# First layer of a two-block network on one core: k, v and the first queries from h without adaLN's shift

## Chip, cores and metric

One core of one Trainium2 chip runs the whole program. The metric is the device time of one execution in microseconds; the table below gives three of them and the one that was profiled.

## Reference

The input x is 256 tokens by 2048 columns, in float32, and there are 256 context tokens of the same width. A first block has two layers, a second block one (a gated spatial and recurrent mix, and a feed-forward part in three pieces); the change is in the first block. Cut to what matters:

```python
shift, scale, gate = jnp.split(jax.nn.silu(c) @ ada_w[l] + ada_b[l], 3, axis=-1)
shift_c, scale_c, gate_c = jnp.split(jax.nn.silu(c_ctx) @ ada_w[l] + ada_b[l], 3, axis=-1)
h = rmsnorm(x, norm_g[l]) * (1.0 + scale[:, None]) + shift[:, None]
hc = rmsnorm(xc, norm_g[l]) * (1.0 + scale_c) + shift_c
q, k, v, up, uf, g = split_proj(h @ w_in[l])     # and the same of hc
```

q and k get a norm per head and, for x's tokens, rope; attention of 8 heads in 2 key groups over 512 keys follows; up and uf go through a pooling and a Fourier mix; the three are joined, multiplied with silu(g), and projected by w_out. Since h is a scaled part plus one row per source, h @ W is the scaled part times W, plus shift @ W added to every row.

## The kernel before

**Chunks.** All weights stream from DRAM in chunks of 512 KB (128 partitions x 1024 float32) through 8 buffers, RAW, loaded in order by SyncE's queue. A chunk of w_in or w_out is split in two float32r parts, SPL (4 buffers): ScalarE copies the high part (L1329), VectorE subtracts to get the low part (L1555), and TensorE does three matmuls (high x high, high x low, low x high) for each product. A chunk of ada_w isn't split: TensorE multiplies it in float32 by the two columns of silu(c) (CW), two matmuls of 128x512 for a chunk, each shown as two records (L1113). Eight chunks of ada_w are one group of 512 of adaLN's 6144 values; a group's result is copied out (ada_out, L1339), turned with TensorE (ada_turn, L1181) and added up on VectorE into the columns ADA. Of the 12 groups of a layer, 0 to 3 are the shift, 4 to 7 the scale and 8 to 11 the gate.

**Buffers come free** at different moments: a RAW buffer of a split chunk when VectorE has taken its low part, one of an ada chunk only when TensorE has multiplied it. A load waits in SyncE's queue for the buffer eight chunks back, with every later load behind it.

**The order** of all engines' work is one list, written when the program is built. `run_chunks` walks the chunks; before each it takes pieces of small work from the list `hi` (or `low`, for attention rows), as many as the chunk group's `side` says: norms, tiles of h, attention, pooling, squares. Every engine does its part of the list in order, so an engine that waits holds all that follows. `run_ahead` places a chunk's split 5 chunks ahead of its multiplication (AHEAD), at the start 3 (START_AHEAD, for the first 72 chunks). Ada chunks that aren't needed at once lie in the list `left`, and `mixed` lays them between the chunks of a projection, two after every second one.

**The start** (`start`, `main`): 64 ada chunks of layer 0, scale and shift of one quarter of the columns at a time, with the 8 chunks of the k and v projection (kv) between them; then q0, q1 (queries), gp (pool), gf (Fourier) and the gates, with `left` between. In between, x and ctx are loaded, turned by TensorE into columns (turn_x, L1167, 16 times, copied by VectorE, L1566), and the mean squares give the row scale (rstd_a, rstd_b: L1572, L1950, L1577, L1174). A tile of h (128 columns of one source, 256 tokens) takes three steps: h0 on VectorE scales (L1599), h1 on ScalarE adds the shift and rounds to the high part (L1347), h2 on VectorE makes the low part (L1604). In layer 1, h1 has a second pass on ScalarE (L1350) and h2 runs on GpSimd (L1959). A chunk of kv, or of the first layer's projections, is 24 matmuls of 512 columns (L1132 to L1134, or L1146 to L1148); in layer 1's q0, q1, gp and gf it is 12.

**kv to q0.** When kv is done, kv_out empties `hi`, in which `load_tables` (three small loads on ScalarE's DMA queue, L1356 to L1358) and `tables` (VectorE, L1615 to L1618) stand, and then copies k to QS and v to VT (L1365, L1371, L1626), which lie where the columns of x were, once these are spilled to DRAM (L1945). q0 uses the same four banks of PSUM. Then the norms run (n0, n1, n2) and attention units of four steps: scores (L1196), softmax, turned probabilities (L1203), times v (L1213).

**Between the layers**, 8 ada chunks (FILL) are laid after w_out's last: four, then the count of the squares (L1265), four more, then the row scale (L1174) and layer 1's first tiles of h.

Of the kernel before, what the change touches and what calls it, by code (L numbers as in the profile page):

```python
# [5 lines left out]
F32 = mybir.dt.float32  # L6
# [15 lines left out]
FILL = 8  # L22
# [35 lines left out]
def two_block_program(nc, I, out):  # L58
    es = ExitStack()
    with es:  # L60
# [57 lines left out]
        gate = lambda l, k, s: ADA[:, l, 32 + k, s:s + 1]  # L118
        V = lambda c: VV[:, c:c + 1]
# [62 lines left out]
        s_h0, s_h1, s_h1b, s_h2 = sem("h_scaled"), sem("h_hi"), sem("h_shifted"), sem("h_lo")  # L182
# [124 lines left out]
        def run_chunks(upto):  # L307
            while at["pos"] < upto:
# [4 lines left out]
                if c.shape == 0:  # L313
                    pop_side(2 if c.group.side == 2 and c.kc % 2 == 0 else 0)
# [5 lines left out]
                ks = {0: [], 2: range(2 * c.kc, 2 * c.kc + 2), 4: range(4 * c.kc, 4 * c.kc + 4)}[c.shape]  # L320
# [3 lines left out]
                for part in range(parts):  # L324
                    if part:
                        pop_side(c.group.side)
# [17 lines left out]
        def mixed(main, left):  # L344
            seq = []
            for c in main:
                seq.append(c)
                if len(seq) % 4 == 2:
                    seq.extend(left[:2])
                    del left[:2]  # L350
            return seq
# [5 lines left out]
        ada_ready, s2_ready = {}, {}  # L357

        def ada_group(l, g, side=0):
            def after():  # L360
# [5 lines left out]
                hi.insert(1, lambda: spread(slot))  # L366

            def spread(slot):
                s = put("ada_turn", slot=slot, l=l, g=g, after=use(7))
# [63 lines left out]
        def tile_h(l, k, s, x, done):  # L433
            y = {}

            def s0():
                y["slot"], last = take()
                y["h"] = put("h0", l=l, k=k, s=s, slot=y["slot"], last=[x["rs"], s2_ready[l, k // 4], *last])["n"]
                bank_last[5] = [(s_h0, y["h"])]

            def s1():
                y["h"] = put("h1", l=l, k=k, s=s, slot=y["slot"], scaled=y["h"], last=[ada_ready[l, k // 4], *x["ended"]])["n"]
                y["again"] = tick("h1b") if l else 0

            def s2():
                h = put("h2", l=l, k=k, s=s, slot=y["slot"], hi=y["h"], again=y["again"])
# [4 lines left out]
        def layer(l):  # L451
            both, lv = l == 0, lay[l]
            W = I["w_in"][l, :, :]
            h, x = {}, {"qs": [], "ended": [], "maps": [[(s_colT, 3)], [(s_colT, 3)]]}
# [6 lines left out]

            def need_x(k):
# [4 lines left out]
            need["kv", l] = need_both  # L467
# [18 lines left out]
            def rows_out(banks, width, queries=False):  # L486
# [3 lines left out]
                elif both or x.get("qs_used"):  # L490
                    flush(hi)
                x["qs_used"] = True
                s = put("rows_out", l=l, banks=banks, width=width, last=[multiplied(), *x["qs"]], a=count.get("qa", 0), d=count.get("qd", 0))
                x["qs"] = []
# [6 lines left out]
            def norm_item(i, nh, which, tt, ready, dest):  # L501
                y = {}
                rope = tt[0] == 0

                def s0():
                    slot, last = take()
                    s = put("n0", l=l, i=i, nh=nh, slot=slot, last=[ready, *last])
                    give(slot, (s_nred, s["n"]))

                def s1():  # L510
                    (a, last), (c, more) = (take(), take()) if rope else ((None, []), (None, []))
                    s = put("n1", l=l, i=i, nh=nh, which=which, t=tt[1], rope=rope, a=a, c=c, last=last + more + [x["tables"]], rope_n=tick("rope") if rope else 0)
# [4 lines left out]
                def s2():  # L517
                    bk = 5 if both else 7
                    s = put("n2", l=l, i=i, nh=nh, dest=dest, bank=bk, after=use(bk))
                    bank_last[bk] = [(s_nev, s["n"])]  # L520
                    x["qs"].append((s_ntr, s["n"]))
                    x["qk"] = (s_nev, s["n"])
                return [s0, s1, s2]

            def kv_out():
# [5 lines left out]
                for b in range(4):  # L531
                    bank_last[b] = [(s_v, 4 * s["n"] - 3 + b)]
                hi.extend(staged([norm_item(i, 2, 1, tt, ready[i], lv.KTr[:, :, i * 128:(i + 1) * 128]) for i, tt in enumerate(TILES)]))
                if not both:
                    hi.append(lambda: low.extend([unit_row] * (2 * len(us) + 3)))
# [156 lines left out]
            kv = group("tm", ("kv", l), W, 1024, [0, 1, 2, 3], kv_out, TILES)  # L692
# [1404 lines left out]
```

## Time and profile before

| what | value |
|---|---|
| median of 3 runs | 2458.5 us (2456.53 to 2460.01) |
| profiled execution | 2454.96 us, its span 2453.2 us |
| busy in the span | PE 2324.8 us (95%), DVE 1291.5 (53%), ACT 1043.2 (43%), POOL 197.1 (8%) |
| DMA | 436.66 MB, mean 178 GB/s |
| a load of ada_w, of w_in | 512 KB each, x192 and x208 |

The span runs from the first to the last instruction; the profiled execution's own time is 1.8 us more. PE is TensorE's matmul, DVE VectorE, ACT ScalarE, POOL GpSimd, SP SyncE; a q behind the name is the engine's queue, where loads are issued. Matmuls overlap each other, so a row's length (0.39 us) is more than the distance between two starts (0.23 us), and it is the starts that are to be counted.

### The profile page before, as it was taken

Reading aid. Unit: us, or ns where it says so; the run is one execution under the profiler, and the core shown is the slowest. Engines: PE = TensorE matmul, PEld = TensorE weight load, DVE = VectorE, ACT = ScalarE, POOL = GpSimd, SP = SyncE. Lnnn points to the kernel's source line nnn. Section 1 sums busy time; section 2 is a strip of 40 time slices with the busy share of each in tenths; the row PEclk is TensorE's granted clock in tenths of the full one; section 3 lists DMA queues with packets and bytes.
Section 4 is the critical chain, followed back from the end, with each engine's and each line's share of the span. In section 5 each row is a group of like instructions: output and inputs, shape, how many; then the busy total and the mean of one; then the engine's idle time right before and its main releaser. Section 6 shows DMA issues by size and latency. Waiting matters only on the chain.

```text
span 2453.2 us, 30580 instructions
## 1 busy us (share of the span) xinstructions
PE 2324.8 (95%) x12135; PEld 1861.9 (76%) x12135; DVE 1291.5 (53%) x2110; ACT 1043.2 (43%) x1596; POOL 197.1 (8%) x237
## 2 busy tenths in 40 slices
PE   5889999999999979899989988989999999999998
PEld 2467777677777657678877867868888888888887
DVE  2444533142332263545666776557665676567664
ACT  2232333342321263445544545445543555345543
POOL 1000100000010131100021014120000000000001
PEclk8999999999999999999989999989999999999999
DMA  9864433335655565534555554646655655565652
GB/s 367 294 236 172 142 120 124 123 112 171 232 172 172 202 221 208 167 102 147 187 157 171 180 172 130 189 132 186 189 181 188 189 183 186 186 186 186 188 184 83
DMA packets 347021, 436.66 MB, mean 178 GB/s; under 512 B 13848, under 2 KB 269280, under 8 KB 345984
## 3 DMA queue, kind: packets, MB, share of 16 engines
q1 hardware_dynamic: 341376, 413.19, 51.8%
q0 software_dynamic: 3408, 16.38, 1.9%
q10 hardware_dynamic: 2096, 5.15, 0.6%
q8 instruction: 96, 1.57, 0.3%
q14 instruction: 45, 0.37, 0.0%
HBM read 428.37 MB, written 6.29 MB: 177 GB/s over the span
## 4 chain that ended last, share of the span: by engine, by line
PE 85%; DVE 5%; ACT 4%; DMA 3%; issue 2%; POOL 1%; SPq 0%; ACTq 0%; POOLq 0%; DVEq 0%
PE ps L1151 32%; PE ps L1152 16%; PE ps L1146 5%; PE ps L1148 5%; PE ps L1147 5%; PE ps L1132 4%; PE ps L1134 4%; PE ps L1133 4%; PE ps L1113 3%; ACT SPL L1329 2%; DVE SPL L1555 2%; PE ps L1196 1%; PE ps L1213 1%; DMA RAW<-in_w_in_dram 1%; DMA RAW<-in_ada_w_dram 1%
## 5 line engine op out<-in xcount | busy, mean ns | idle before, releaser
L1151 PE MATMUL ps<-HS,SPL 128*128 128x512 f32 x3456 | 1236.1, 402 | 16.9 <-POOL HS L2007 16.1
L1555 DVE TENSOR_TENSOR SPL<-RAW,SPL 128x1024 fp32r<-128x1024 f32 x592 | 726.4, 1233 | 669.4 <-ACT SPL L1329 667.3
L1152 PE MATMUL ps<-HS,SPL 128*128 128x256 f32 x3456 | 973.6, 282 | 0.0
L1329 ACT ACTIVATE SPL<-RAW 128x1024 fp32r<-128x1024 f32 x592 | 621.7, 1057 | 536.1 <-PE ps L1152 356.5
L1151 PEld LDWEIGHTS ps<-HS,SPL 128*128 128x128 f32 x3456 | 654.6, 189 | 183.4 <-POOL HS L2007 16.9
L1152 PEld LDWEIGHTS ps<-HS,SPL 128*128 128x128 f32 x3456 | 658.2, 190 | 2.1 <-issue 1.9
L1132 PE MATMUL ps<-SPL,HS 128*128 128x512 f32 x576 | 248.5, 431 | 30.1 <-ACT XT L1371 8.5
L1134 PE MATMUL ps<-SPL,HS 128*128 128x512 f32 x576 | 228.5, 397 | 0.0
L1133 PE MATMUL ps<-SPL,HS 128*128 128x512 f32 x576 | 228.4, 396 | 0.0
L1146 PE MATMUL ps<-HS,SPL 128*128 128x512 f32 x512 | 212.2, 414 | 1.2 <-DVE HS L1711 1.2
L1148 PE MATMUL ps<-HS,SPL 128*128 128x512 f32 x512 | 200.5, 392 | 0.0
L1147 PE MATMUL ps<-HS,SPL 128*128 128x512 f32 x512 | 200.2, 391 | 0.0
L1132 PEld LDWEIGHTS ps<-SPL,HS 128*128 128x128 f32 x576 | 110.4, 192 | 79.6 <-issue 22.1
L2002 POOL TENSOR_TENSOR TMP<-TMP 128x256 f32<-128x256 f32 (+1 forms) x68 | 61.6, 905 | 1240.5 <-ACT TMP L1463 1238.0
L1133 PEld LDWEIGHTS ps<-SPL,HS 128*128 128x128 f32 x576 | 110.8, 192 | 26.6 <-issue 6.0
L1146 PEld LDWEIGHTS ps<-HS,SPL 128*128 128x128 f32 x512 | 96.6, 189 | 43.9 <-issue 16.1
L1134 PEld LDWEIGHTS ps<-SPL,HS 128*128 128x128 f32 x576 | 110.3, 192 | 24.8
L1113 PE MATMUL ps<-RAW,CW 128*32 128x512 f32 x768 | 113.6, 626 | 11.2 <-DMA RAW<-in_ada_w_dram 9.1
L1463 ACT ACTIVATE TMP<-XT 128x256 f32<-128x256 f32 (+1 forms) x72 | 33.5, 465 | 191.9 <-DVE XT L1723 124.1
L1147 PEld LDWEIGHTS ps<-HS,SPL 128*128 128x128 f32 x512 | 96.7, 189 | 22.4 <-issue 3.8
L1148 PEld LDWEIGHTS ps<-HS,SPL 128*128 128x128 f32 x512 | 96.4, 188 | 21.1
L1908 DVE SCALAR_TENSOR_TENSOR MM<-MM,VV 128x256 f32<-128x256 f32 x192 | 80.0, 478 | 0.0
(251 smaller groups left out, 1543.7 us busy)
## 6 DMA issues: line engine op xcount, KB each, us to landing
RAW<-in_w_in_dram SPq DMA_DIRECT2D x208, 512.0 KB, 5.6
RAW<-in_ada_w_dram SPq DMA_DIRECT2D x192, 512.0 KB, 4.9
RAW<-in_ffn_w_up_dram SPq DMA_DIRECT2D x192, 512.0 KB, 3.6
RAW<-in_w_out_dram SPq DMA_DIRECT2D x96, 512.0 KB, 4.5
RAW<-in_ffn_w_down_dram SPq DMA_DIRECT2D x96, 512.0 KB, 3.4
x_spill<-XT POOLq DMA_DIRECT2D x2, 2048.0 KB, 14.8
XT<-x_spill POOLq DMA_DIRECT2D x1, 4096.0 KB, 15.8
MM<-in_x_dram ACTq DMA_DIRECT2D x2, 1024.0 KB, 10.8
```

What stands on the lines that cost most here:

```text
L1113: m = mm(PS[6][32 * q:32 * q + 32, :], CW[:, 2 * k:2 * k + 32], raw_of(i)[:, kk * 512:(kk + 1) * 512], start=kc < 2, stop=kc >= 6, skip_gr ...
L1132: mm(PS[b][:, :], hr, wr, start=k == 0, stop=False, skip_group_check=True)
L1133: mm(PS[b][:, :], hr, wl, start=False, stop=False, skip_group_check=True)
L1134: m = mm(PS[b][:, :], hl, wr, start=False, stop=k == KT - 1, skip_group_check=True)
L1146: mm(PS[b][:, :], wr, hr, start=k == 0, stop=False, skip_group_check=True)
L1147: mm(PS[b][:, :], wr, hl, start=False, stop=False, skip_group_check=True)
L1148: m = mm(PS[b][:, :], wl, hr, start=False, stop=k == KT - 1, skip_group_check=True)
L1151: mm(PS[b][:, :], wr, hh, start=k == 0, stop=False, skip_group_check=True)
L1152: m = mm(PS[b][:, 256:512], wl, hh[:, 0:256], start=False, stop=k == KT - 1, skip_group_check=True)
L1329: act(SPL[:, (n - 1) % NSPL, 0, :], raw_of(i), ACT.Copy).then_inc(s_hi, 1)
L1555: tt(w[:, 1, :], raw_of(s["i"]), w[:, 0, :].bitcast(F32), ALU.subtract).then_inc(s_lo, 1)
L1908: stt(o, CV[c][:, tap:tap + 256], V(c_fw[tap] + col), o, ALU.mult, ALU.add).then_inc(s_ct, 1)
```

## The change

It does the following.

1. kv and q0 of layer 0 read a "bare" h: scaled and split, without the shift (`tile_h`, ACT.Copy in h1). So `start` holds only the four scale groups (32 ada chunks) and kv. The four shift groups move behind it (`go_on`), between the 8 chunks of q0, and when a quarter of the shift is there, `shift_h` adds it to that quarter's tiles: the same three steps again for the 32 tiles, from the high and low parts.
2. The missing part of k, v and q0 is a row: `shift_rows` multiplies the shift columns with the chunks of w_in's columns 1024 to 1535 and 0 to 511, **loaded a second time**: 16 more chunks in ada form, laid between q1's chunks, two after each. The row is spread over the tokens by two float32 matmuls of 512 columns for each of the two groups, and VectorE adds it to the four tiles of rows, which wait in BARE (MM's memory). k's norms come after the first, q0's after the second; attention starts behind that.
3. `kv_out`'s emptying of `hi` is gone for layer 0: kv's banks are copied at once, in full width; `load_tables` and `tables` stand in `hi` behind the last tiles of h.
4. h2 of layer 1 goes from GpSimd to VectorE, and the second ScalarE pass of h1 goes.
5. START_AHEAD now holds to chunk 80. In layer 0 from q1 on, a half chunk takes a piece of `hi` and one of `low`, no longer one of them. During the first scale group six pieces are taken at every second chunk, no longer two.
6. `left` is laid out anew: none between q1's chunks, two after each chunk of w_out (before: after every second), FILL is 16, and none remains for layer 1's projections, which had 24.

```diff
-FILL = 8
+FILL = 16
+        BARE = [MV[:, i, 8:16, :].rearrange("p k n -> p (k n)").rearrange("p (t c) -> p t c", t=4) for i in range(2)]
-            while at["taken"] < min(len(queue), at["pos"] + (START_AHEAD if at["pos"] < 72 else at["ahead"])):
+            while at["taken"] < min(len(queue), at["pos"] + (START_AHEAD if at["pos"] < 80 else at["ahead"])):
...
+                    hi.insert(1, lambda: add(slot, s["n"]))
+                def add(slot, out):
+                    while "scr_a" not in x:
+                        hi.pop(0)()
+                    s = put("shift_rows", which=which, slot=slot, out=out, ready=x["bare"][which], last=x["scr_a"], after=use(4, 5))
...
-            kv = group("tm", ("kv", l), W, 1024, [0, 1, 2, 3], kv_out, TILES)
-            q0 = group("tm", ("in", l), W, 0, qb[0], q_out(0, qb[0]), lv.tiles, 1 if both else 2)
+            kv = group("tm", ("kv", l), W, 1024, [0, 1, 2, 3], bare_out(0) if both else kv_out, TILES)
+            q0 = group("tm", ("kv", l), W, 0, qb[0], bare_out(1), TILES) if both else group("tm", ("in", l), W, 0, qb[0], q_out(0, qb[0]), lv.tiles, 1 if both else 2)
...
-                cs = ada_group(0, 4 + u, 2) + ada_group(0, u, 2)
+                cs = ada_group(0, 4 + u, 2 if u else 6)
...
-                return cs[:12] + kv[2 * u - 2:2 * u - 1] + cs[12:] + kv[2 * u - 1:2 * u] if u else cs
+                return cs[:4] + kv[2 * u - 2:2 * u - 1] + cs[4:] + kv[2 * u - 1:2 * u] if u else cs
+            def go_on(u):
+                c = q0[2 * u + 1]
...
+                    hi.extend(staged([shift_h(k, s, bare, h, used) for k in range(4 * u, 4 * u + 4) for s in range(2)]))
...
+                cs = ada_group(0, u, 2)
+                return cs[:4] + q0[2 * u:2 * u + 1] + cs[4:] + [c]
...
-                main = [c for u in range(4) for c in start(u)] + kv[6:8], q0 + q1 + gp + gf + gates
+                main = ([c for u in range(4) for c in start(u)] + kv[6:8] + [c for u in range(4) for c in go_on(u)]
+                        + mixed(q1, shift_rows(0) + shift_rows(1), 1)), gp + gf + gates
...
-        lay_out(mixed(outs0, left))
+        lay_out(mixed(outs0, left, 1))
...
-        run_chunks(marks[1] + FILL // 2)
-        at["ahead"] = 2
+        run_chunks(marks[1] + 6)
...
-        run_chunks(marks[2])
+        run_chunks(marks[1] + 12)
+        flush(hi)
+        at["ahead"] = AHEAD
...
-                    if l:
-                        e.wait_ge(s_h1, n)
-                        act(t, t, ACT.Identity, bias=shift(l, k, src)).then_inc(s_h1b, 1)
...
+                elif kind == "shift_rows":
+                    for sm, v in new((s_sel, 16)):
+                        e.wait_ge(sm, v)
+                    e.wait_ge(s_adaE, s["out"])
+                    for src in range(2):
+                        m = mm(PS[4 + src][:, :], SPREAD[:, src, :], T(s["slot"]), start=True, stop=True, skip_group_check=True)
+                    m.then_inc(s_sp, 1)
```

## Rows read from the trace of the kernel before

**Rows 1.** Page of the profile: busy us of each engine, share of the span, instructions.

```profile
PE 2324.8 (95%) x12135; PEld 1861.9 (76%) x12135; DVE 1291.5 (53%) x2110; ACT 1043.2 (43%) x1596; POOL 197.1 (8%) x237
```

**Rows 2.** Windows table: us, busy us of each engine, granted clock, DMA share, GB/s.

```profile
20.00:40.00 20.00, 16.53 (x91) 6.61 (x88) 6.62 (x17) 5.20 (x6) 0.00 (x0) 0.71 1.05 390
0.00:160.00 160.00, 112.61 (x567) 60.64 (x568) 58.69 (x139) 44.34 (x70) 12.47 (x26) 0.90 0.91 331
210.00:272.00 62.00, 61.26 (x309) 46.06 (x307) 32.87 (x69) 22.38 (x42) 4.93 (x4) 1.00 0.38 135
845.00:1000.00 155.00, 132.68 (x630) 92.69 (x622) 77.96 (x136) 73.55 (x122) 36.66 (x41) 0.96 0.64 223
```

**Rows 3.** Timeline, 20 to 75 us: start, length, engine, line, tile, wait.

```profile
23.78 1.91 ACT L1334 ACTIVATE HS<-MM 128x2048 fp32r<-128x2048 f32 x1 [1.27 <-DMA MM<-in_ctx_dram]
...
32.94 1.09 PE L1167 MATMUL ps<-IDN,MM 128*128 128x128 f32 x8
...
34.96 1.09 PE L1167 MATMUL ps<-IDN,MM 128*128 128x128 f32 x8
...
58.69 0.68 DVE L1566 COPY XT<-ps 128x512 f32<-128x512 f32 x1
...
66.26 0.47 PE L1132 MATMUL ps<-SPL,HS 128*128 128x512 f32 x1 [0.65 <-DVE HS L1604]
...
72.80 1.93 PE L1113 MATMUL ps<-RAW,CW 128*32 128x512 f32 x16
```

**Rows 4.** Timeline of TensorE, 118 to 137 us.

```profile
121.69 0.50 PE L1132 MATMUL ps<-SPL,HS 128*128 128x512 f32 x1 [2.65 <-DVE SPL L1555]
...
127.36 1.92 PE L1113 MATMUL ps<-RAW,CW 128*32 128x512 f32 x16
...
129.21 0.50 PE L1132 MATMUL ps<-SPL,HS 128*128 128x512 f32 x1
```

**Rows 5.** Timeline, 140 to 163 us, and landing times of GX's small loads.

```profile
143.55 0.53 ACTq L1358 DMA_DIRECT2D GX<-in_k_norm_g_dram  x1
...
153.38 0.43 DVE L1615 TENSOR_TENSOR XT<-TMP,GX 128x256 f32<-128x256 f32 x1 [10.33 <-DMA GX<-in_k_norm_g_dram]
...
155.15 0.75 DVE L1626 COPY XT<-ps 128x256 f32<-128x256 f32 x2
...
156.79 0.77 PE L1132 MATMUL ps<-SPL,HS 128*128 128x512 f32 x1 [8.12 <-ACT XT L1371]
...
161.19 0.52 PE L1133 MATMUL ps<-SPL,HS 128*128 128x512 f32 x1
...
DMA to landing us min/median/max: 5.2/7.2/9.8
```

**Rows 6.** Timeline of TensorE, 205 to 215 us: q1's first matmul.

```profile
208.99 0.47 PE L1132 MATMUL ps<-SPL,HS 128*128 128x512 f32 x1 [0.59 <-DVE XT L1626]
```

**Rows 7.** Chain that ended last, 230 to 250 us and 780 to 860 us.

```profile
240.11 0.86 PE ps L1196 x2
...
820.63 1.00 PE ps L1113 x8
...
832.73 1.00 PE ps L1113 x8
```

**Rows 8.** Timeline, 830 to 860 us: the boundary between the two layers.

```profile
849.48 0.88 SPq L1080 DMA_DIRECT2D RAW<-in_w_in_dram  x2
...
853.04 1.06 ACT L1329 ACTIVATE SPL<-RAW 128x1024 fp32r<-128x1024 f32 x1 [5.36 <-DMA RAW<-in_w_in_dram]
...
858.38 0.47 PE L1132 MATMUL ps<-SPL,HS 128*128 128x512 f32 x1 [2.26 <-POOL HS L1959]
```

**Rows 9.** Who waited for whom on TensorE: us in total, times, longest us.

```profile
PE ps L1132 <- POOL HS L1959: 7.0, 5, 3.8
```

**Rows 10.** Timeline of VectorE, 104 to 130 us: two steps of h.

```profile
107.85 0.48 DVE L1599 SCALAR_TENSOR_TENSOR TMP<-XT,S,ps 128x256 f32<-128x256 f32 x1
...
108.24 0.48 DVE L1604 SCALAR_TENSOR_TENSOR HS<-TMP,ADA,HS 128x256 fp32r<-128x256 f32 x1
```

More of the change, by code:

```diff
@@ L313, in run_chunks @@
                 if c.shape == 0:
[L314 removed]
+                    pop_side(c.group.side if c.kc % 2 == 0 else 0)
                 elif c.group.side == 0:
@@ L324, in run_chunks @@
                 for part in range(parts):
-                    if part:
+                    if part and c.group.side == 0:
+                        pop_pair()
+                    elif part:
                         pop_side(c.group.side)
@@ L342, in staged, with mixed @@
             return [row(r) for r in range(len(tasks) + depth - 1)]
-        def mixed(main, left):
+        def mixed(main, left, every=2):
             seq = []
[L346 to L350, printed above, removed]
+            for i in range(0, len(main), every):
+                seq.extend(main[i:i + every] + left[:2])
+                del left[:2]
             return seq
@@ L357, in two_block_program, with need_shift @@
         ada_ready, s2_ready = {}, {}
+        need["ada"] = lambda k: [(s_c, 1)]
+        def need_shift(k):
+            while any((0, g) not in ada_ready for g in range(4)):
+                hi.pop(0)()
+            return [ada_ready[0, g] for g in range(4)]
+        need["shift"] = need_shift
         def ada_group(l, g, side=0):
@@ L460, in need_both, with need_bare @@
                 return [h[k, 0], h[k, 1]]
+            def need_bare(k):
+                while (k, 1) not in bare or (k, 0) not in bare:
+                    hi.pop(0)()
+                return [bare[k, 0], bare[k, 1]]
             def need_x(k):
@@ L465, in need_x @@
                 return [h[k, 0]]
-            need["kv", l] = need_both
+            need["kv", l] = need_bare if both else need_both
             need["in", l] = need_both if both else need_x
@@ L489, in rows_out, with copy_rows @@
                         hi.pop(0)()
-                elif both or x.get("qs_used"):
+                elif x.get("qs_used"):
                     flush(hi)
                 x["qs_used"] = True
-                s = put("rows_out", l=l, banks=banks, width=width, last=[multiplied(), *x["qs"]], a=count.get("qa", 0), d=count.get("qd", 0))
-                x["qs"] = []
+                while "tab" not in x:
+                    hi.pop(0)()
+                last, x["qs"] = [multiplied(), *x["qs"]], []
+                return copy_rows(banks, width, [lv.QS[:, i, 0:width] for i in range(len(banks))], last)
+            def copy_rows(banks, width, dest, last):
+                put("rows_out", banks=banks, width=width, dest=dest, last=last)
                 ready = []
@@ L506, in s0 @@
                     slot, last = take()
-                    s = put("n0", l=l, i=i, nh=nh, slot=slot, last=[ready, *last])
+                    s = put("n0", l=l, i=i, nh=nh, rows=xq, slot=slot, last=[ready, *last])
                     give(slot, (s_nred, s["n"]))
@@ L511, in s1 @@
                     (a, last), (c, more) = (take(), take()) if rope else ((None, []), (None, []))
-                    s = put("n1", l=l, i=i, nh=nh, which=which, t=tt[1], rope=rope, a=a, c=c, last=last + more + [x["tables"]], rope_n=tick("rope") if rope else 0)
+                    s = put("n1", l=l, i=i, nh=nh, rows=xq, which=which, t=tt[1], rope=rope, a=a, c=c, last=last + more + [x["tables"]], rope_n=tick("rope") if rope else 0)
                     if rope:
@@ L724, in start_h, with add_shift @@
                         put("spill", last=[multiplied()])
[L725 to L726 removed]
+                    hi.extend(staged([tile_h(0, k, s, x, bare) for k in range(4 * u, 4 * u + 4) for s in range(2)])
+                              + ([lambda: put("select_in"), load_tables, tables, load_dft] if u == 3 else []))
                 cs[-1].then = start_h
[L728 removed]
+                return cs[:4] + kv[2 * u - 2:2 * u - 1] + cs[4:] + kv[2 * u - 1:2 * u] if u else cs
+            def go_on(u):
+                c = q0[2 * u + 1]
+                after_q = c.then
+                def add_shift():
+                    while (0, u) not in ada_ready:
+                        hi.pop(0)()
+                    used = multiplied()
+                    hi.extend(staged([shift_h(k, s, bare, h, used) for k in range(4 * u, 4 * u + 4) for s in range(2)]))
+                    if after_q:
+                        after_q()
+                c.then = add_shift
+                cs = ada_group(0, u, 2)
+                return cs[:4] + q0[2 * u:2 * u + 1] + cs[4:] + [c]
             def begin():
```

130 lines of the change are left out of this document (93 added, 37 removed).

## The prediction

> **What bounds the kernel now.** The page comes first: TensorE is busy for 2324.8 of 2453.2 us, VectorE for 1291.5 [rows 1], so time is won where TensorE stands idle and lost where its work grows. The windows table says where: in the first 160 us it is busy for 112.6, at a mean granted clock of 0.90, while DMA is 0.91 busy; from 210 to 272 us it is busy for 61.3 of 62.0; from 845 to 1000 us, where layer 1 begins, for 132.7 of 155 [rows 2]. So there is idle time at the start and in layer 1, and next to none between. The timelines say why. The first kv matmul comes at 66.26 us, since the columns of x are turned a few at a time between ada chunks (last copy at 58.69) [rows 3]; then 64 ada chunks have to be loaded, twice as many as the scale needs; and at the end of kv VectorE waits 10.3 us for a small load, and TensorE 8.1 us behind it [rows 5].
>
> **The start.** The last part of ctx is there at 23.8 us. Two turns and two ada chunks take 2.02 us now, a pair of turns alone 1.09 [rows 3]. Sixteen turns with six chunks between them so take between 8.7 and 16.2 us; I take 12.5, nearer the mixed row. From the last copy to the first matmul it is 7.6 us (58.69 to 66.26) [rows 3], and the scale's last group has to be turned first (1.1 us). So kv begins at 23.8 + 12.5 + 7.6 + 1.1 = 45.0 us.
>
> From there TensorE sets the pace. A kv chunk takes 5.67 us, a block of four ada chunks 1.85 [rows 4], together 7.52; their five loads take 5 x 1.34 = 6.7 us at 390 GB/s [rows 2]. DMA keeps up, with 10% to spare. The first chunk takes 6.5 us [rows 3], then come five times 7.52, three turns of a group (0.6 each), 1.8 us of waiting for the last quarter's tiles (an estimate: two tiles, each two steps 0.395 apart [rows 10]) and two more kv chunks: 45.0 + 6.5 + 37.6 + 1.8 + 1.8 + 11.3 = 104.0 us.
>
> Here the stall of kv's end is **kept, and grows**. By my count of the pieces, `load_tables` and `tables` are both taken at the first ada chunk behind kv, and kv's copies stand before them. ScalarE copies two banks of 512 columns (1.3 us; two of 256 take 0.75) and issues three loads (the last takes 0.53, so 1.6), that one lands 5.2 to 9.8 us later, VectorE works on the tables for 1.8 us (153.4 to 155.2) [rows 5], and q0's first split (1.2 us) stands behind that in VectorE's order. I take 7.2 for the landing, the middle of the loads read: the deep queue of spill and loads that gave 9.8 is mostly gone by then. q0 begins at 104.0 + 1.3 + 1.6 + 7.2 + 1.8 + 1.2 = 117.1 us; with four ada chunks done in between, TensorE idles for 11.2 us. Before, 8.1.
>
> The Trainium skill (DMA: Bandwidth & Descriptors, "Queues, rings and completion order") says that each DMA engine serves the queues in turn, packet by packet, so a small load on ScalarE's queue needn't wait until SyncE's large ones are through. The 9.8 us of the trace speak against relying on it. By that rule the landing would be at the short end, and the sum 2 us lower.
>
> q0: eight chunks, seven blocks of four, four turns of a group, and 2.2 us for the lower clock after the stall, as from 156.79 to 161.19 us, where starts are 0.43 us apart and no longer 0.23 [rows 5]: 45.4 + 13.0 + 2.4 + 2.2 = 63.0. With 0.7 us for the first copy, q1 begins at 180.8 us, and not at 208.99 [rows 6]: 28.2 us earlier. What was done by then and now isn't goes off: four pairs of `left` and k's turns (1.2 us). Two ada chunks are 1.00 us busy; with the change to and fro I price a pair at 1.2, since two pairs in w_out's stage are 12.10 us apart, with 48 matmuls 0.227 apart between them [rows 7]. So 28.2 - 4.8 - 1.2 = **22.2 us won**. The second set of 32 tiles costs VectorE 32 x 2 x 0.395 = 25 us and ScalarE 16 [rows 10]; it lies beside q0's 63 us, where VectorE otherwise has 10 of splits. I cost it at nothing; uncovered, it would hold q1.
>
> **What is added.** The 16 chunks of w_in loaded again go between q1's chunks, where TensorE is full [rows 2]: eight pairs, **9.6 us lost**. DMA has 135 GB/s there and hides them. Spreading the rows: four float32 matmuls of 512 columns at 0.86 (scores have that shape) [rows 7], **3.4 lost**. VectorE's additions (some 6 us) lie beside q1 and gp. The attention rows now start in gp's last chunk; the last that a gate wants (unit 32, row 35) is taken some 20 half chunks before need, so I put nothing for them.
>
> **`left`.** The gates lose eight pairs, w_out's stage gains sixteen, both full [rows 2, 7]: **9.6 lost**. The fill gains eight chunks, layer 1's projections lose twelve pairs: **14.4 won** if TensorE sets the pace there.
>
> **The boundary.** Fills 8 to 15 can be loaded only when fills 0 to 7 are multiplied, and layer 1's first chunk of w_in comes behind them. From the first fill (about 849 us) a load takes 3.6 us to the split (849.5 to 853.04 [rows 8]), eight more are ahead at 1.34: 863.3, plus 2.6 of split is 865.9, and not 858.38: **7.5 lost**.
>
> **h2 on VectorE.** TensorE's waits for GpSimd's h2 go, **7.0 won** [rows 9]. VectorE then needs 2 x 2 x 0.395 + 1.23 = 2.8 us for a chunk of q0 with x's tiles alone, about TensorE's 2.8 (half of 5.67), but 4.4 where ctx's tiles are made too, in four chunks (6.8 us over), and the tables (2.3) stand before them: **9.1 lost**. The windows row's clock of 0.96 over 155 us [rows 2] means 6 us lost to low clock; with shorter pauses I give 2.3 back. Layer 1 with its boundary: -14.4 + 7.5 - 7.0 + 9.1 - 2.3 = -7.1.
>
> **Sum:** -22.2 + 9.6 + 3.4 + 9.6 - 7.1 = -6.7 us. Against the profiled execution's 2454.96 this is 2448.3; that one lies 3.5 below the median of the three runs, and I carry the difference to the median: 2452 us.
>
> **Bounds.** Turns -3.8 to +3.7; landing -2.0 to +2.6; a pair 1.0 to 1.4, with 16 more pairs in full stages, 3 either way; layer 1's VectorE from nothing (-9) to as much again (+7); the start's loads: at the 331 GB/s mean of the first 160 us [rows 2] five loads take 7.9 us and not 6.7, 0.4 more than TensorE's 7.52, 13 times: +5.
>
> **Rivals.**
> A. *The start pays in full and VectorE keeps up in layer 1.* Landing 5.2 us, turns at their short end, no shortage by h2: 2452 - 2 - 3.8 - 9.1 = 2437 us. For it: VectorE is busy for 78 of 155 us there [rows 2]. Against: its work comes in bursts in front of need. 0.22.
> B. *Slower: the pairs moved out of layer 1 are paid twice.* While idle time there comes from the in-order splits and tiles of h, ada chunks fill it for nothing; in w_out's stage each pair costs 1.2. It decides once VectorE's 4.4 us for a chunk stands against TensorE's 2.8: then the 14.4 us don't come back, and the time is 2452 + 14 = 2466 us. For it: TensorE idles 22 us there with these fillers in. Against: k and v's eight chunks of 5.67 leave VectorE ample time, so their four pairs do come back. 0.22.
> C. *The start stays bound by its loads.* Twice four of eight buffers wait for TensorE's multiplications, the spill falls into kv's end, and q1 begins near 191, not 181: 2462 us. 0.12.
> D. *It doesn't do what it says*, as tables that hold q0 until the spill is done, or h that is late for q1, eat the start's gain: 2458, no change. 0.06.
> The forecast has 0.38, with 2445 to 2459 as its own range.
>
> **How the numbers follow.** A measurement of this kernel can tell about 0.2%, 4.9 us, from no change. Faster by more (under 2453.6): A and 0.25 of the forecast's 0.38, together 0.47. Within: 0.13 of the forecast, D, and parts of B and C, 0.27. Slower (over 2463.4): most of B and half of C, 0.26. The range, 2436 to 2468, takes in A's and B's times.
>
> **What would show it.** In the profile after: first kv matmul near 45 us; a wait of VectorE for GX's load and one of TensorE of 10 to 12 us behind it near 105 to 117 us; q1 near 181; the ada line with 832 records (208 chunks of four), no longer 768; TensorE full from q1 to w_out; layer 1's first matmul 21 us after w_out's last, no longer 14; TensorE waiting there for VectorE's h. I am wrong if q1 begins before 172 or after 190, if the boundary costs under 3 us, or if layer 1's stretch from there to the pool projection is shorter than before by more than 12 us.

## The result and the profile after

| | before | after |
|---|---|---|
| median of the runs compared | 2459.26 us (2456.53 to 2463.38) | 2489.74 us (2483.93 to 2495.43) |
| span of the profiled execution | 2453.2 us | 2482.1 us |

The ratio is **1.0137, 95% interval 1.0109 to 1.0165**: slower by 30 us, outside the range. The runs below were compared in later groups, each against its own runs of the kernel before (medians 2456.13, 2454.69, 2455.32, 2453.45), so ratios are what to compare.

The windows table of the profile after (columns as in [rows 2]) has the start better and the rest worse:

```profile
0.00:160.00 160.00, 119.24 (x631) 77.40 (x635) 70.38 (x167) 47.55 (x80) 12.38 (x26) 0.96 0.84 301
186.00:642.00 456.00, 446.76 (x2132) 327.20 (x2130) 171.26 (x342) 142.23 (x242) 22.60 (x25) 1.00 0.42 140
845.00:1000.00 155.00, 122.43 (x513) 85.17 (x512) 77.39 (x144) 47.71 (x72) 8.10 (x7) 0.86 0.53 176
```

The timeline of the start, after. kv begins 21.2 us sooner than in [rows 3], TensorE's wait in front of q0 is longer than in [rows 5], and q1 comes 23.3 us sooner than in [rows 6]:

```profile
45.09 0.47 PE L1219 MATMUL ps<-SPL,HS 128*128 128x512 f32 x1 [2.16 <-DVE HS L1703]
...
115.09 0.43 DVE L1729 TENSOR_TENSOR XT<-TMP,GX 128x256 f32<-128x256 f32 x1 [8.50 <-DMA GX<-in_k_norm_g_dram]
...
118.21 0.76 PE L1219 MATMUL ps<-SPL,HS 128*128 128x512 f32 x1 [11.09 <-DVE SPL L1650]
...
134.42 0.42 ACT L1443 ACTIVATE HS<-TMP 128x256 fp32r<-128x256 f32 x1 [5.54 <-PE ps L1221]
134.75 1.04 ACT L1424 ACTIVATE SPL<-RAW 128x1024 fp32r<-128x1024 f32 x1
137.10 0.50 PE L1219 MATMUL ps<-SPL,HS 128*128 128x512 f32 x1 [0.92 <-DVE SPL L1650]
...
142.45 1.06 ACT L1424 ACTIVATE SPL<-RAW 128x1024 fp32r<-128x1024 f32 x1 [1.30 <-DMA RAW<-in_w_in_dram]
...
185.73 0.47 PE L1219 MATMUL ps<-SPL,HS 128*128 128x512 f32 x1 [1.64 <-DVE MM L1740]
```

The timeline of TensorE at the boundary, after, which answers to [rows 8]. The first row is w_out's last matmul, the last one layer 1's first. Between them lie 18 ada chunks, not 16: the last pair that is laid among w_out's chunks stands behind its last matmul (863.12), and the turn of its group waits for its copy before the first fill starts at 866.73. The kernel before has the same, and so 10 chunks there and not 8:

```profile
862.80 0.39 PE L1235 MATMUL ps<-HS,SPL 128*128 128x512 f32 x1
863.12 1.06 PE L1200 MATMUL ps<-RAW,CW 128*32 128x512 f32 x8
866.17 0.63 PE L1276 MATMUL ps<-IDN,TMP 128*128 128x128 f32 x4 [1.99 <-ACT TMP L1434]
866.73 4.48 PE L1200 MATMUL ps<-RAW,CW 128*32 128x512 f32 x24
...
874.83 3.93 PE L1200 MATMUL ps<-RAW,CW 128*32 128x512 f32 x16 [0.74 <-ACT TMP L1434]
...
884.08 3.28 PE L1200 MATMUL ps<-RAW,CW 128*32 128x512 f32 x8 [1.66 <-DMA RAW<-in_ada_w_dram]
892.48 1.08 PE L1276 MATMUL ps<-IDN,TMP 128*128 128x128 f32 x4 [5.12 <-ACT TMP L1434]
893.21 0.77 PE L1219 MATMUL ps<-SPL,HS 128*128 128x512 f32 x1
```

The same timeline of the kernel before, from w_out's last matmul to the first matmul of layer 1's gates, and that second matmul after:

```profile
844.45 0.39 PE L1148 MATMUL ps<-HS,SPL 128*128 128x512 f32 x1
...
1063.84 0.79 PE L1151 MATMUL ps<-HS,SPL 128*128 128x512 f32 x1
```

```profile
1099.30 0.79 PE L1238 MATMUL ps<-HS,SPL 128*128 128x512 f32 x1
```

With the start of ScalarE's first pass for w_out (647.04 before, 642.70 after) the path falls into four stretches, and they say where the time went:

| stretch | before | after | difference | I had predicted |
|---|---|---|---|---|
| start to w_out | 647.0 | 642.7 | -4.3 | -18.8 |
| w_out, to its last matmul | 197.4 | 220.1 | +22.7 | +19.2 |
| to layer 1's first matmul | 13.9 | 30.4 | +16.5 | +7.5 |
| to layer 1's gates | 205.5 | 206.1 | +0.6 | -14.6 |

Together +35.5 at layer 1's gates; the rest is 6.6 us shorter, for no reason in the change: that tail is 1381 to 1391 us long in all profiled executions here, in no order with the edits. (The last column puts each term of the prediction in the stretch that it lies in.)

### The profile page after: what moved, and what is told of

It is laid out like the page before. It is cut to its first block, busy times and chain, and to the rows that moved or that the text cites. A ratio compares the mean times of both kernels' runs of the same rounds, so it can differ in the third digit from the quotient of the medians.

```text
span 2482.1 us, 30820 instructions
## 1 busy us (share of the span) xinstructions
PE 2335.6 (94%) x12207; PEld 1864.3 (75%) x12207; DVE 1330.8 (54%) x2218; ACT 1036.7 (42%) x1592; POOL 172.6 (7%) x206
## 4 chain that ended last, share of the span: by engine, by line
PE 84%; DVE 6%; ACT 4%; issue 2%; DMA 2%; POOL 1%; ACTq 0%; POOLq 0%; DVEq 0%
PE ps L1238 31%; PE ps L1239 15%; PE ps L1233 5%; PE ps L1234 5%; PE ps L1235 5%; PE ps L1219 4%; PE ps L1221 4%; PE ps L1220 4%; PE ps L1200 3%; ACT SPL L1424 2%; DVE SPL L1650 2%; PE ps L1291 1%; PE ps L1308 1%; PE ps L1298 1%; PE ps L1334 1%
## 5 line engine op out<-in xcount | busy, mean ns | idle before, releaser
L1238 PE MATMUL ps<-HS,SPL 128*128 128x512 f32 x3456 | 1229.1, 400 | 17.9 <-POOL HS L2121 16.9
L1219 PE MATMUL ps<-SPL,HS 128*128 128x512 f32 x576 | 247.7, 430 | 35.7 <-DVE SPL L1650 14.4
L1200 PE MATMUL ps<-RAW,CW 128*32 128x512 f32 x768 | 106.7, 628 | 4.6 <-ACT CW L1414 2.0
```

The lines of the kernel that those rows point to most:

```text
L1200: m = mm(PS[6][32 * q:32 * q + 32, :], vec, raw_of(i)[:, kk * 512:(kk + 1) * 512], start=kc < 2, stop=kc >= 6, skip_group_check=True)
L1219: mm(PS[b][:, :], hr, wr, start=k == 0, stop=False, skip_group_check=True)
L1238: mm(PS[b][:, :], wr, hh, start=k == 0, stop=False, skip_group_check=True)
```

## The experiments

**Undo the layout of `left`** (e1_left). Fillers are the ada chunks laid between others. Here 24 are back in layer 1's projections, 48 between w_out's chunks and not 64, FILL and the boundary's code as before.

```diff
-FILL = 16
+FILL = 8
-        lay_out(mixed(outs0, left, 1))
+        for i, c in enumerate(outs0):
+            seq.append(c)
+            if i % 4 < 3:
+                seq.extend(left[:2])
+                del left[:2]
...
-        run_chunks(marks[1] + 6)
+        run_chunks(marks[1] + FILL // 2)
+        at["ahead"] = 2
```

> The changed kernel with layer 1's fillers put back: FILL 8 with the old code at the boundary, 24 chunks of left in layer 1's projections again, and so 48 instead of 64 between w_out's chunks. Theory (the boundary and the missing fillers lose most of layer 1's 19 us): w_out's last matmul to layer 1's first falls from 30.4 us to 14 to 16, w_out's stage is 9 us shorter, layer 1 gets 12 pairs back of which its idle time takes a half, in all 12 to 20 us faster than the changed kernel, 2470 to 2478 us. Rival (h2 on VectorE is the cause of layer 1's loss): the boundary still falls, but layer 1's stretch grows by the whole 12 to 14 us, in all no more than 8 us faster. Rival of the record (pairs are paid wherever they lie): the same time for left, only the boundary gains.

Measured: 2460.02 us, a ratio to the kernel before of 1.0020 (1.0010 to 1.0031). By the ratios the layout alone is 29 of the 34 us lost, and more than the 12 to 20 I expected. Its boundary is 13.1 us long, and its layer 1, 24 fillers richer, 200.2 us, no longer than after's.

**Undo the move of h2**, alone (e2_pool) and together with the above (e3_both): h1's second pass on ScalarE and h2 on GpSimd again.

```diff
+                        act(t, t, ACT.Identity, bias=shift(l, k, src)).then_inc(s_h1b, 1)
...
-                elif kind == "h2":
...
+                elif kind == "h2" and s["l"] == 0:
...
+                    e.wait_ge(s_h1b, s["again"])
+                    tt(HX(1, k, src, 1), T(s["slot"])[:, 0:256], HX(1, k, src, 0).bitcast(F32), ALU.subtract).then_inc(s_h2, 1)
```

> The changed kernel with layer 1's h2 back on GpSimd and h1's second pass back on ScalarE. Theory (the boundary and fillers): VectorE is relieved of 32 x 0.4 = 13 us, TensorE's waits for h (7.6 us) and for the norms (12.9 us) shrink to those of the kernel before (7.0 and 7.0), 3 to 7 us faster than the changed kernel; the boundary stays at 28 us or more. Rival (h2 on VectorE is the cause): 12 us or more faster.

> Both together: what is left of the change is layer 0's start, the shift rows, and a row of attention per half chunk. Theory: about the sum of the two alone, 15 to 25 us faster than the changed kernel, 2465 to 2475 us, so still slower than the kernel before by 6 us or more, because the 16 extra chunks and 9 us of waits in q1, gp and gf eat what the start wins. Rival (the whole loss is in layer 1): at or below 2459 us.

Measured: 2493.4, 1.0158 (1.0143 to 1.0173), and 2462.82, 1.0023 (1.0007 to 1.0039). Nothing is won by undoing it, where I had expected 3 to 7 us for it alone; if anything it is a little worse. Who waited for whom on TensorE, 860 to 1010 us, after and then with h2 on GpSimd: the wait for h changes its name and hardly its length.

```profile
PE ps L1283 <- DVE MM L1770: 10.6, 2, 5.6
PE ps L1219 <- DVE HS L1705: 7.6, 5, 2.3
PE ps L1276 <- ACT TMP L1434: 7.1, 2, 5.1
PE ps L1219 <- DVE MM L1740: 4.6, 1, 4.6
```

```profile
PE ps L1284 <- DVE MM L1770: 11.8, 2, 6.1
PE ps L1220 <- POOL HS L2073: 9.8, 7, 3.6
PE ps L1277 <- ACT TMP L1435: 7.5, 2, 5.5
PE ps L1220 <- DVE MM L1740: 4.4, 1, 4.4
```

**Issue the tables' loads early**, when the spill is placed, in front of the last quarter's tiles; on the kernel after (e4_early), and on the first experiment's (e5_start).

```diff
                     if u == 3:
                         put("spill", last=[multiplied()])
+                        fetch_tables()
...
```

> The changed kernel with the three small loads of layer 0's tables issued right after the spill's place in the order, before the last quarter's tiles, instead of behind kv's copies. Theory (the in-order wait for that load holds q0's first split): VectorE's wait of 8.8 us and TensorE's 11.1 us at 107 to 118 us are gone, q0 begins near 108, and 7 to 11 us are won, 2479 to 2483 us. Rival (the wait only stands in front of late loads): TensorE waits for loads of w_in and ada_w there instead, and 3 us or less are won.

> Layer 1's fillers and FILL 8 put back (as in e1_left), and layer 0's table loads issued early (as in e4_early). Theory (the two losses are independent): e1_left's 2460 less the 6 to 10 us that the early loads won, 2450 to 2454 us, 2 to 6 us faster than the kernel before. Rival (what is won at the start is lost again in front of later loads): 2457 to 2461 us, no faster than before.

Measured: 2483.34, 1.0116 (1.0101 to 1.0131), and **2451.7, 0.9985** (0.9970 to 1.0001). The timeline of the second shows that the wait in front of q0 shrinks from 11.09 us to 2.67, and that q0 begins 6.7 us sooner than after:

```profile
111.56 0.47 PE L1230 MATMUL ps<-SPL,HS 128*128 128x512 f32 x1 [2.67 <-DVE SPL L1661]
```

By the medians that is 6 and 8 us of the time, by the ratios 5 and 9. So the stall was predicted in its place and size, and it was the change's to avoid.

**The change's small edits without its idea**: on the kernel before, turns six at a time and early tables together (e6_base), then each alone (e10_turns, shown below, and e11_tables).

```diff
-                    pop_side(2 if c.group.side == 2 and c.kc % 2 == 0 else 0)
+                    pop_side(c.group.side if c.kc % 2 == 0 else 0)
-                cs = ada_group(0, 4 + u, 2) + ada_group(0, u, 2)
+                cs = ada_group(0, 4 + u, 2 if u else 6) + ada_group(0, u, 2)
```

> The kernel before with two of the change's small parts and none of its rows: the columns of x turned six at a time in the first group, and the table loads issued early. If TensorE's idle time of the old start comes from the late turns and the table wait, kv's first matmul comes at 46 us and not 66, the 8.1 us in front of q0 go, and 10 us or more are won, 2446 us or less. If the old start is bound by its 72 loads (which would be done at 125 us if they never paused), the turns win 2 to 4 us and the table wait gives 5 to 8, 2446 to 2450 us. If neither helps, 2455 us or more.

> The kernel before with one thing of the change alone: in the first scale group six pieces are taken at every second chunk, not two, so that the columns of x are turned sooner. In e6_base this stood together with earlier tables and gave 2451.7 against 2454.7, but the first kv matmul was no earlier (67.3 against 66.3), for 16 ada chunks are loaded in front of it. If loads set kv's start, nothing: 2454 to 2456. If the turns do, 2 to 4 us: 2451 to 2453.

> The kernel before with the three small loads of the tables issued as soon as the spill is placed, ahead of the last quarter's tiles of h, and nothing else. The wait of VectorE for GX (10.3 us) and of TensorE behind it (8.1) should go and only one for the k and v copies stay, some 1 to 2 us: 6 us fewer at q0. If the time saved there is kept, 2449 to 2451; if e6_base's 3 us is all that it gives, since TensorE then meets the loads of q0's chunks sooner, 2451 to 2453; if it is given back whole, 2455.

Measured: 2451.73, 0.9987 (0.9969 to 1.0006); 2454.38, 0.9997 (0.9980 to 1.0015); 2451.49, 0.9988 (0.9974 to 1.0002). None can be told from no change, but e6_base stands where the change stands with its layout mended and its tables early (2451.7). The early turns don't bring kv's start to 46 us, as one branch of the expectation had it: it is at 67.27 with both edits and at 64.28 with the turns alone, not 66.26. In e6_base the chain in front of it is two waits for loads of ada_w (6.68 and 9.71 us), so loads and not turns held it. With the early tables alone, q0 begins at 156.81 us and before at 156.79. TensorE waits 4.65 us now, not 8.12, but kv ends 3.5 us later, and the small loads came late all the same (below).

**Mend only the boundary (e7_fill8), or only the fillers (e14_fill16).** The one keeps 64 ada chunks between w_out's and has 8 left for layer 1, with the boundary's code as before; the other keeps after's boundary of 16 and has 40 and 24.

```diff
-FILL = 16
+FILL = 8
...
```

```diff
-        lay_out(mixed(outs0, left, 1))
+        for i, c in enumerate(outs0):
+            seq.append(c)
+            if i % 8 in (0, 1, 3, 4, 6):
+                seq.extend(left[:2])
+                del left[:2]
+        lay_out(seq)
```

> The changed kernel with FILL 8 and the old code at the boundary, but still two chunks of left after each of w_out's; the eight that are over go between the first of layer 1's chunks. Tells the boundary from the missing fillers. Theory (the boundary, where sixteen loads stand in a row): its 30.4 us fall to 14 to 17, and 14 to 18 us of the 28 that e1_left won come back, 2472 to 2476 us. Rival (layer 1 wants its fillers): the boundary falls as well, but q0, q1 and kv of layer 1 grow by the same, 2482 us or more. If both matter little once the loads flow, 2462 us.

> The kernel after with 24 ada chunks back in layer 1's projections, taken from w_out's stage (40 in place of 64), but its boundary as it is: 16 fills, and the row scale placed behind the twelfth. The counterpart of e7_fill8, which mended the boundary alone and gave 18 of the 28 us. If the two parts add, 2490 - 10 = 2480. If the long boundary is also what starves layer 1's first chunks, so that fillers there can't be loaded in time either, the gain is under 5 us: 2485 to 2490. If the missing fillers are what makes the boundary costly, over 15 us: under 2475.

Measured: 2471.14, 1.0066 (1.0045 to 1.0086), and **2464.25, 1.0047** (1.0031 to 1.0062). Against after that is -17 and -22 us by the ratios, and -29 for both: the parts overlap. The timelines say what each did. w_out's last matmul, layer 1's first and its gates' first, with the boundary mended and then with the fillers mended:

```profile
861.90 0.39 PE L1235 MATMUL ps<-HS,SPL 128*128 128x512 f32 x1
...
879.17 0.47 PE L1219 MATMUL ps<-SPL,HS 128*128 128x512 f32 x1 [1.29 <-DVE HS L1705]
...
1082.60 0.79 PE L1238 MATMUL ps<-HS,SPL 128*128 128x512 f32 x1
```

```profile
846.55 0.39 PE L1241 MATMUL ps<-HS,SPL 128*128 128x512 f32 x1
846.86 2.78 PE L1206 MATMUL ps<-RAW,CW 128*32 128x512 f32 x24
...
868.59 1.09 PE L1282 MATMUL ps<-IDN,TMP 128*128 128x128 f32 x4 [3.31 <-ACT TMP L1440]
869.33 0.78 PE L1225 MATMUL ps<-SPL,HS 128*128 128x512 f32 x1
...
1071.07 0.79 PE L1244 MATMUL ps<-HS,SPL 128*128 128x512 f32 x1
```

The boundary mended: 17.3 us in place of 30.4, w_out's stage as long as after's. The fillers mended: w_out's last matmul 16.3 us sooner for 11 pairs fewer in front of it, the boundary 22.8 us, and layer 1, with 12 pairs in it, 201.7 us and not 206.1. The fills' own code is after's, yet the boundary is 7.6 us shorter. Of this 3.6 are the layout's: no pair stands behind w_out's last matmul now, and the first fill starts 0.3 us behind it, not 3.9. Then, after, the first 24 matmul records of the fills take 4.48 us and here 2.78, and the copy of the last ada group (ada_out) is waited for 5.12 us and here 3.31.

**Layer 1 takes the fillers for nothing.** The same stretch in all sixteen profiled kernels, by what was laid in it:

| ada chunks among layer 1's projections | from its first matmul to its gates, us |
|---|---|
| 0 | 204.6, 206.1, 207.2 |
| 8 | 203.4 |
| 24 | 200.2, 201.7, 204.0, 204.3, 204.7, 205.3, 205.5, 205.9, 206.0, 207.2 |
| 32 | 201.0, 203.7 |

and w_out's stage, by the chunks in front of its last matmul:

| ada chunks among w_out's | to its last matmul, us |
|---|---|
| 24 | 193.9 |
| 30 (32 laid) | 195.8, 195.8, 197.4, 197.4 |
| 40 | 204.7, 204.7 |
| 48 | 208.2, 209.7, 209.7, 209.8, 209.8 |
| 62 (64 laid) | 220.0, 220.1, 220.1, 220.1 |

The second table rises by 26.2 us over 19 pairs, 1.38 a pair; the first doesn't rise at all. The windows table says why, for 142 us from layer 1's first matmul, before, after, and with 24 fillers and 16 fills:

```profile
858.00:1000.00 142.00, 124.08 (x558) 88.21 (x558) 72.86 (x121) 68.59 (x114) 33.87 (x39) 0.95 0.62 217
```

```profile
893.00:1035.00 142.00, 115.37 (x459) 90.20 (x458) 79.97 (x148) 49.00 (x77) 10.06 (x9) 0.89 0.39 119
```

```profile
869.00:1011.00 142.00, 127.65 (x582) 91.56 (x581) 84.02 (x157) 54.33 (x85) 11.15 (x9) 0.96 0.63 223
```

Without fillers TensorE does less and isn't done sooner: it is idle for 27 us, not 14 to 18, waits there for VectorE's norms (5.00 and 5.55 us at one turn each), and runs at a granted clock of 0.89, not 0.95. The two other kernels without fillers (e2_pool, e4_early) have 0.89 in this stretch too, and e7_fill8, with 8, has 0.93. Directly behind the boundary it starts a matmul every 0.43 us, at 1.2 GHz, where 0.23 is what it does at 2.4:

```profile
893.79 0.63 PE L1220 MATMUL ps<-SPL,HS 128*128 128x512 f32 x1
894.21 0.63 PE L1221 MATMUL ps<-SPL,HS 128*128 128x512 f32 x1
894.64 0.63 PE L1219 MATMUL ps<-SPL,HS 128*128 128x512 f32 x1
```

The Trainium skill (TensorE: Matmul & The Clock Gate, "Part 1: The HAM clock gate") says that the gate sets the clock by how busy TensorE has been recently. The rows agree: of the three stretches shown, the one with most idle time has the lowest clock. So a filler there gets its time back from two sources, idle time that it fills and a clock that stays up; how much each gives was not measured apart.

**More of the same.** Eight more chunks from w_out's stage to layer 1's, on the change with mended layout and early tables (e12_more), and on the kernel before with early tables alone (e13_plain).

```diff
-            if i % 4 < 3:
+            if i % 8 in (0, 1, 3, 4, 6):
```

```diff
-        lay_out(mixed(outs0, left))
...
+            if i % 8 in (1, 3, 6):
...
```

> e5_start with 8 more of the left ada chunks in layer 1's projections (32 in place of 24) and 8 fewer between w_out's (40 in place of 48). From e7_fill8, with 8, to e1_left, with 24, eight pairs moved there gave 10 to 11 us. If that goes on, four pairs more give 4.8 us: 2447 beside e5_start's 2451.7, and faster than the kernel before beyond doubt. If the idle time that pays for them lies in the first 24 chunks of layer 1 alone, the last four pairs (between the chunks of gp) cost there what they save, and it is 2451 to 2453.

> e11_tables (the kernel before with earlier tables, none of the rows) with 8 more of the left ada chunks in layer 1's projections (32 in place of 24) and 8 fewer between w_out's (24 in place of 32). e12_more did the same on top of the change's start and gave 2445.6, 6 us under e5_start. If that gain belongs to layer 1 alone, it comes here too: 2445 to 2447, and the bare h with its rows is worth nothing at all. If it needs layer 1's h2 on VectorE, which shortens its waits, the fillers cost here what they save: 2451, and the change's parts are worth 5 us together.

Measured: **2445.57, 0.9954** (0.9938 to 0.9970), and **2441.92, 0.9950** (0.9935 to 0.9964). Both beat both kernels clearly, and the second has nothing of the bare h in it. Its timeline has w_out's last matmul 4.8 us sooner than before, the boundary at 12.4 us, and layer 1 at 201.0:

```profile
839.69 0.39 PE L1159 MATMUL ps<-HS,SPL 128*128 128x512 f32 x1
...
852.05 0.47 PE L1143 MATMUL ps<-SPL,HS 128*128 128x512 f32 x1 [2.04 <-POOL HS L1970]
...
1053.07 0.79 PE L1162 MATMUL ps<-HS,SPL 128*128 128x512 f32 x1
```

**The price of the rows**, and of an attention row per half chunk. The first kernel (e9_two, on e1_left) multiplies only the first two chunks of each shift group, so that the added rows lack the part of 14 of h's 16 column tiles; the second (e8_single, on e1_left too) sets `side` to 1 again for gp, gf and the gates.

```diff
-                return group("ada", "shift", W, (1024, 0)[which], [6], after)
+                cs = group("ada", "shift", W, (1024, 0)[which], [6], after)
+                cs[1].then, cs[-1].then = after, None
+                return cs[:2]
```

```diff
-            side = 0
+            side = 1 if both else 0
```

> e1_left with only the first two chunks of each of the two shift groups, so 12 of the 16 chunks of w_in that are loaded a second time are left out (the rows added to k, v and q0 lack the part of 14 of the 16 column tiles of h); the spreading and the additions stay. If a pair of them costs 1.2 us between q1's chunks, as I priced it, six pairs fewer are 7.2 us: 2453 beside e1_left's 2460. If they cost more than their own matmuls, because their loads and buffers hold q1's chunks (TensorE stood idle for some 7 us more between 186 and 380 us than before the change), it is 10 to 14 us: 2446 to 2450. If q1's stage is held by something else, such as VectorE's shifted tiles of h, under 5 us.

> e1_left with the old rule in gp, gf and the gates of layer 0: a half chunk takes one piece, of hi or of low. The attention rows then wait for the pool's and the Fourier mix's pieces, and at the gates that need them they have to be taken one right behind the other, with nothing between them for TensorE. Theory: 8 to 20 us slower than e1_left, with waits of TensorE at turned probabilities and scores; so the pair rule is worth having here. Rival (the rows side by side are what costs the 9 us in gf): faster than e1_left by 3 us or more.

Measured: 2455.03, 0.9994 (0.9979 to 1.0009), and 2466.36, 1.0044 (1.0022 to 1.0067). Six pairs fewer give 5.0 us by the medians and 6.4 by the ratios (1.0020 less 0.9994, times 2456), but with the intervals of both that is anything from 2 to 11. The stretch that they lie in is steadier: from q1's first matmul to ScalarE's first pass for w_out it is 457.0 to 457.1 us in all nine profiled kernels with the change and its attention rule, and 455.8 in e9_two. The windows table has that stretch with all eight pairs (e1_left), then with two:

```profile
186.01:643.01 457.00, 447.07 (x2132) 327.48 (x2132) 171.85 (x343) 143.10 (x244) 22.63 (x25) 1.00 0.41 140
185.38:641.21 455.83, 441.67 (x2084) 328.00 (x2084) 171.46 (x343) 140.06 (x241) 20.65 (x25) 1.00 0.38 126
```

TensorE does 5.4 us less and is idle 4.2 us more; its largest wait there is for VectorE's norms (4.2 us in four turns, the longest 2.3). So by the trace the six pairs cost their stretch 1.2 us in all, not 7.2: a stretch in which TensorE is 98% busy also gives back little of what is taken out. The attention row per half chunk is worth some 6 us to the change, less than the 8 to 20 expected; the same stretch is 464.3 us long without it.

## Why the prediction was wrong

**The step that failed** is the one under `left`: "layer 1's projections lose twelve pairs: 14.4 won if TensorE sets the pace there". It doesn't. Layer 1's stretch came out 0.6 us longer without the twelve pairs, and with 0, 24 or 32 fillers it is the same. This is rival B's mechanism, to which I gave 0.22: idle time from the in-order work of other engines, which fillers use for nothing. Its condition, that VectorE's h be too slow for TensorE, isn't borne out: moving h2 back changed nothing, and the longest waits there are for VectorE's norms. [Rows 2] had the evidence: 22 us of idle time in 155 and a clock of 0.96. I saw idle time left over there and still took TensorE's work for what sets the pace; the fillers stood in room that would else be idle too.

**The boundary** was another, 16.5 us and not 7.5. From the first fill to layer 1's first split I had 14.3 us (863.3 less 849), and it was 20.0 (866.73 to 886.77). I counted the loads that stand before it. What I left out: the fills' own matmuls at low clock (3.93 us for four chunks, where [rows 3] have 1.93), and that the last fills' copy stands in ScalarE's order behind four splits of layer 1, each waiting for its load, so that its turn holds TensorE for 5.12 us:

```profile
886.77 1.06 ACT L1424 ACTIVATE SPL<-RAW 128x1024 fp32r<-128x1024 f32 x1 [3.23 <-DMA RAW<-in_w_in_dram]
...
891.75 0.58 ACT L1434 ACTIVATE TMP<-ps 128x512 f32<-128x512 f32 x1
```

**The start**, point by point:
- kv at 45.1 (45.0 predicted), its rows out at 105.3 (104.0): right, and not by terms that cancel (ctx's last part at 24.5, not 23.8, and the last copy starts 12.0 us behind it, not 12.5).
- The stall: 11.09 us of idle time (11.2), the small load 8.8 us from issue to landing (7.2), q0 at 118.2 (117.1): right.
- q1 at 185.7 and not 180.8, inside the 172 to 190 I had named. From q0's first matmul on, TensorE is busy for 63.0 us, as predicted, and idle for 4.5, where I had 0.7. Three times it waits 0.92 us for a split (the first at 137.10), and each time ScalarE has done that split right behind the first shifted tile of a quarter, for which it had waited for TensorE (134.42). Then 1.64 us go for VectorE's copy of q0's rows. One split of q0 waits for its load (142.45), and TensorE doesn't wait behind it.
- From q1 to w_out the change was to cost 9.4 us more than what was there before, and it cost 18.9. The windows have TensorE idle for 9.2 of 456 us there, and before for 2.6 of 438 (435.42 busy), so 6.7 us are idle time where "TensorE is full" was my ground for the pairs' price; the waits listed there are many and short (1.7 us in total the most of any, 1.6 the longest), for VectorE's copies and norms above all. The reloaded chunks, priced at 9.6, are not what is dear there: six of the eight pairs cost 1.2 us together. The spreading took 3.8 us of TensorE and not 3.4. What sets the pace of this stretch was not found.
- The shifted tiles of h, costed at nothing beside q0's 63 us, stand by the rows above in front of 2.8 us of TensorE's waits in q0. Whether those splits could have been made sooner without them no run shows.
- The eight pairs that "the gates lose" lay between q0's and q1's chunks; behind q1 both kernels have 48 ada chunks up to w_out. The sum is the same.

**h2 on VectorE**: 7.0 won and 9.1 lost by the prediction (its 6.8 for four chunks should be 6.4, four times 4.4 less 2.8), nothing that the runs can tell from zero either way. The wait for h stays, whoever makes it.

**w_out's stage**: 16 pairs more, 19.2 predicted, 22.7 measured, 1.42 each and 1.38 over the whole table. Every fourth pair also brings its group's turn of 0.6 us, 0.15 a pair, and I priced a pair from two that are 12.10 us apart and hold no turn.

Summed by stretch: 14.5 us at the start, 3.5 in w_out's stage, 9.0 at the boundary and 15.2 in layer 1 are what I was short of; the tail gave 6.6 back.

**Does the idea pay?** With its layout mended and its tables early it is at 2451.7, beside 2451.5 for the kernel before with early tables; with eight more chunks in layer 1 it is 0.9954 and 0.9950. q1's 23 us are all spent again, 18.9 of them between q1 and w_out: by the reloaded chunks, the spreading and the pairs that the start no longer hides as work, and by idle time. Since leaving out most of the reloaded chunks returned 1.2 us, the price lies in the order of the work rather than its amount; another order of norms and rows was not tried.

## What to carry to other kernels

Filler work must lie where the engine idles anyway: price the place it leaves and the place it goes to separately, and take idle time in the windows table as room that is used or usable, not as cost to be saved by taking work away. Even 98% busy is no proof that TensorE's work sets the pace: take some of it out and see whether the stretch gets shorter. At the seam of two stages, count what the last filler's copy stands behind in its engine's order. And when a change bundles an idea with small edits and a new layout, run the small edits and layouts on the old kernel first: here one of each, early tables and four pairs moved into layer 1, were worth 12 us there, and the idea nothing more that could be measured.

## What the runs showed of the hardware

A small load can take as long to land as the large ones beside it. GX's loads of 64 KB landed 5.3 and 8.8 us after issue in the kernel after. Issued early on the kernel before (e11_tables), between the spill of 2 x 2 MB and SyncE's loads, the same two took 18.1 and 20.1 us, as long as loads eight times their size. The DMA issues in the profile of that kernel, 125 to 150 us (last columns: KB each, median us from issue to landing):

```profile
x_spill<-XT POOLq DMA_DIRECT2D x2, 2048.0 KB, 15.4
RAW<-in_w_in_dram SPq DMA_DIRECT2D x5, 512.0 KB, 19.5
RAW<-in_ada_w_dram SPq DMA_DIRECT2D x4, 512.0 KB, 17.3
TMP<-in_k_rope_dram ACTq DMA_DIRECT2D x1, 256.0 KB, 15.1
GX<-in_q_norm_g_dram ACTq DMA_DIRECT2D x1, 64.0 KB, 18.1
GX<-in_k_norm_g_dram ACTq DMA_DIRECT2D x1, 64.0 KB, 20.1
```

The kernel e5_start issues them early too, beside the same spill (88 to 90 us). There GX's loads took 12.6 and 17.9 us, next to 17.4 and 19.9 for loads of 512 KB, but the 256 KB load that was issued ahead of them in the same queue, and ahead of the spill, took only 7.0. So neither the size nor the traffic settles it alone. What else does, such as the place in the order of issue, these rows don't separate: the load in that place took 15.1 us in e11_tables.

By the rule of the Trainium skill that the prediction weighed (DMA: Bandwidth & Descriptors, "Queues, rings and completion order"), a queue of its own would have brought these small loads in ahead of the large ones; in e11_tables it didn't. The same section says one thing more, which the prediction left out: the write that tells a semaphore of a transfer's end lands only after every earlier write of its DMA engine, over all queues. GX's rows agree with that: these small loads are told of as late as the large ones beside them. Whether their data lay there sooner no run shows.
